# Second feed-forward stage: where the offset and scale of the middle layer norm are applied to the stored residual rows

## The chip, the cores and the metric

The kernel runs on one core of one Trainium2 chip. The metric is device microseconds (us) of one execution. The kernel before takes 2586.59 us (median of 3 runs, 2585.88 to 2588.91). In the text PE is TensorE, DVE is VectorE, ACT is ScalarE, POOL is GpSimd and SP is SyncE, whose queue issues all the DMAs that matter here.

## The reference, cut to what matters

One layer of a transformer-like backbone acts on 1152 rows (1024 latent tokens and 128 context tokens) of width 1024: a feed-forward part, a token mixer, a second feed-forward part, each closed by a layer norm over the residual.

```python
x = layer_norm(ALPHA * x + 0.5 * g1 * swiglu(x * (1.0 + sc1) + sh1, w_f1_in, w_f1_out), ln_g[0], ln_b[0])
y, aux = mixer(x * (1.0 + sc2) + sh2)
x = layer_norm(ALPHA * x + g2 * y, ln_g[1], ln_b[1])
x = layer_norm(ALPHA * x + 0.5 * g3 * swiglu(x * (1.0 + sc3) + sh3, w_f2_in, w_f2_out), ln_g[2], ln_b[2])
```

The change is about the third line and how its result reaches the fourth. Write z for the normalised row, (v - mean) / std. The layer norm's result is z * ln_g[1] + ln_b[1]. It is used twice: as the input of the second feed-forward (for which ln_g[1] and ln_b[1] are folded into per-column factors, so that the feed needs z alone), and as the residual ALPHA * x, which is needed only at the very end, when the last layer norm is made. Matrix products are made in float32 quality by splitting each operand in a high and a low float16 part ("hi" and "lo") and adding three products.

## The kernel before, in words

The 1152 rows are nine tiles (t = 0 to 8) of 128 rows in the buffer Y, 128 x 1024 float32 each. The program's third part (`ffn_phase` with the tag ffn2) begins with the mixer's output projection (class `MixOut`) and goes on with the second feed-forward. Each engine has its own instruction list, written out by hand; the order in a list is fixed, and semaphores are waited for by count. So an engine that waits holds back everything behind it in its own list.

**The opening.** PE makes the output projection tile by tile (L1600). DVE gates it, adds the residual, takes the statistics (`sums`), POOL makes 1/std (`pool`, L1767 and L1768), and DVE makes z in place (`unit`, L1705). PE turns z (L143), ACT and DVE scale it and split it into `act_hi` and `act_lo` (class `Feed`, L165, L170, L184). In between and afterwards, DVE applies the residual's scale and offset to z in place: `affine` (L1708 to L1715) makes two instructions a tile, z * gB (L1714) and + bB (L1715), where gB and bB are ALPHA * ln_g[1] and ALPHA * ln_b[1] spread over all partitions. Tile 0 is done in `vector`, tiles 1 to 5 between the parts of group 0, tiles 6 to 8 in group 1, between its second and third `product`. `store_rows` (L1563) then writes each tile to `x_after_2` in HBM; SP waits for `affined` before each store. Y is then free for the feed-forward's sums.

**The feed-forward.** The hidden width of 2816 is cut into 22 blocks of 128, two blocks (GB) to a group, eleven groups (NG). For each block PE multiplies all rows with two weight columns ("up", L2217 in groups 0 to 2 and 10; a scheme with fewer products, the quarter groups, L2310, in groups 3 to 9), ACT makes SiLU, DVE multiplies and takes maxima (`product`, L2718 and L125), and scales are found from the largest values (`hidden_max`, `hidden_scale`, `win_scale`). A group's "down" products (L2263) are made one group later, in 18 half tiles; DVE adds each to Y (`add`, L2751 for the first, L2753 for the others). Three PSUM banks serve the half tiles in turn, so PE can be three ahead of DVE's adds.

In group 1 PE's list is: up of block 2 for three column chunks, with `spread_h` and `spread_win` (L120) after the first one, which need DVE's `hidden_max` and `win_max` of what came before; `spread_win`; the down products of group 0; up of block 3. DVE's list for it is in `group` (L2760): win_max, product, hidden_scale, win_scale, hidden_lo (L2742), win_lo, product, `mix.affine(dve, 6, 7, 8)`, product, win_scale, and then the eighteen adds. In a quarter group (`quarter_group`, L2858) DVE runs joins (L2829), `low_pieces` (L2855), gates (L2836, L2843), the weights' low parts (L2677, L2673), `hidden_rows`, and the adds.

**POOL.** After the feed is split, POOL makes sums of the operands for the quarter groups (`sums`, L1979 to L2000), and then three instructions for each of the blocks 6 to 19 (`weight_sums`, L2013, L2016, L2019), each set waiting for the set of weights (`raw_in`), for `in_lo` of the block before and for `w_max`. ACT's `win_hi` (L2460) waits for them. At the end POOL gates and merges rows (`Ending.pool`).

**SP.** In each group (L2098) SP waits for `in_lo`, loads a block of input weights, stores rows if any, waits for the next `in_lo`, loads the next block, waits for `out_lo`, and loads two blocks of output weights. The rows of `x_after_2` are read again only in the last group (L1821). The gate rows of the ending are loaded in the opening (L1807).

Of the kernel before, what the change touches and what calls it, by code (L numbers as in the profile page):

```python
# [69 lines left out]
class Plan:  # L70


    def __init__(self, nc, base):
        self.nc, self.at = nc, base
# [117 lines left out]
class Modulation:  # L192
# [177 lines left out]
    def group(self, i):  # L370

        return self.K.mod[:, i * KT:(i + 1) * KT, :]
# [1163 lines left out]
class MixOut:  # L1536


    def __init__(self, K, nc, place, banks, w_at, row_at, feed_at, res_at):
        self.K, self.nc = K, nc  # L1540
# [10 lines left out]
        self.gate = place("mixout_gate_rows", [P, 2, D])  # L1551
        self.gB, self.bB = place("mixout_ln_g_rows", [P, D]), place("mixout_ln_b_rows", [P, D])
        self.xs = [fixed(f"residual_{i}", [P, D], res_at + 4096 * i) for i in range(2)]
# [6 lines left out]
        self.bn, self.rstd, self.z = sem("bn_done"), sem("rstd_done"), sem("z_done")  # L1560
        self.affined, self.x2_stored = sem("rows_affine"), [sem("rows_stored"), sem("last_rows_stored")]

    def store_rows(self, sp, *tiles):  # L1563

        for t in tiles:
            sp.wait_ge(self.affined, t + 1)
            sp.dma_start(self.K.x2_rows(t), self.K.Y[:, t, :]).then_inc(self.x2_stored[t // 6], 16)
# [139 lines left out]

    def affine(self, dve, *tiles):  # L1708

        Y = self.K.Y  # L1710
        for t in tiles:
            dve.wait_ge(self.feeds[t // 6].turned, KT if t // TPC != 1 else 2 * KT)
            dve.wait_ge(self.z, t + 1)
            self.link(self.nc.vector.tensor_tensor(Y[:, t, :], Y[:, t, :], self.gB[:], ALU.mult))  # L1714
            self.nc.vector.tensor_tensor(Y[:, t, :], Y[:, t, :], self.bB[:], ALU.add).then_inc(self.affined, 1)  # L1715

    def vector(self, dve, win_max, win_scale, win_lo):
# [12 lines left out]
        for c, t in ((0, 3), (1, 6)):  # L1730
            self.gated(dve, t, 0, 1)
            self.sums(dve, t)
            if c == 0:
                win_lo(0, 0)
                win_scale(1, 1)
            self.residual(dve, t + 1)
            self.unit(dve, t)
            rest(c, 0, 1)
            self.gated(dve, t + 1, 0)
            rest(c, 2, 3)  # L1740
            self.gated(dve, t + 1, 1)
            self.sums(dve, t + 1)
            rest(c, 4, 5)
            self.residual(dve, t + 2)
            self.unit(dve, t + 1)
            self.gated(dve, t + 2, 0)
            rest(c, 6, 7)
            if c == 0:
                win_lo(1, 1)
            self.gated(dve, t + 2, 1)  # L1750
            self.sums(dve, t + 2)
            self.residual(dve, t + 3)
            if c == 0:
                dve.wait_ge(self.affine_rows, 32)
                for rows in (self.gB, self.bB):
                    self.link(self.nc.vector.tensor_scalar(rows[:], rows[:], ALPHA, None, ALU.mult))
            else:
                self.affine(dve, 0)
            self.unit(dve, t + 2)
# [157 lines left out]


START = 3

# [116 lines left out]
def ffn_phase(nc, K, place, banks, tag, w_in, w_out, unit_i, first=False, out_dst=None):  # L2037

    with ExitStack() as ctx:
# [20 lines left out]
        hfac = place(f"{tag}_h_factor", [P, GB])  # L2060
        mod = qkv = att = end = mix = quarters = None
        if first:
# [5 lines left out]
        else:  # L2068
            end = Ending(K, nc, tag, place, 2, 8, out_dst, spare_at)
            mix = MixOut(K, nc, place, banks, wout_at, odd_at, odd_at + 4 * GB * TOK, end.gated_at)  # L2070
            quarters = Quarters(K, nc, tag, GB * START, GB * (NG - 1 - START), ((end.gated_at + 12288, end.gated_at + 16384), (end.rows_at, end.rows_at + 8192),
                                                              (mix.free_at + 16384, nc.sbuf_usable_end), (mix.free_at, mix.free_at + 8192), (mix.free_at + 8192, mix.free_at + 16384)), spare_at, end.gated_at)
        pa, pu, py = banks[0:2], banks[2:4], banks[4:7]
        h_all, w_all = banks[7][:, 0:P], [banks[7][:, P:2 * P], banks[7][:, 2 * P:3 * P]]
# [15 lines left out]
        def _(sp):  # L2090
# [6 lines left out]

            def group(i, early=(), rest=()):  # L2098
                sp.wait_ge(in_lo, i * GB + 2)
                load_in(i * GB + 3, 1)  # L2100
                mix.store_rows(sp, *early)
                sp.wait_ge(in_lo, i * GB + 3)
                load_in(i * GB + 4, 0)
                mix.store_rows(sp, *rest)
                sp.wait_ge(out_lo, i * GB + GB)
                for b in range(GB):
                    load_out(i * GB + (GB + b), b)

            def late(done):
# [44 lines left out]
            if mix:  # L2154
                end.load_gates(sp)
                mix.load_late(sp)
# [7 lines left out]
            if mix:  # L2164
# [3 lines left out]
                for b in range(GB):  # L2168
                    load_out(b, b)
                mix.store_rows(sp, 0, 1, 2, 3)  # L2170
            if mod:
# [5 lines left out]
            else:  # L2177
                group(0, rest=(4, 5))
                group(1, early=(6, 7, 8))
                for i in range(2, NG - 2):  # L2180
                    group(i)
            sp.wait_ge(in_lo, NB - 2)
# [10 lines left out]
            else:  # L2193
                sp.wait_ge(quarters.products, quarters.PER * quarters.blocks)
                end.load_rows(sp)
                end.load_residuals(sp)
                end.store(sp)
# [451 lines left out]
        def _(dve):  # L2649
# [110 lines left out]
            def group(i, par, n, fresh=False, last=False, at=None, late=None, brackets=False, rows=False):  # L2760
# [13 lines left out]
                product(i, par, 0, 1)  # L2774
                if rows:
                    mix.affine(dve, 6, 7, 8)
                product(i, par, 0, 2)
# [150 lines left out]
            def last_group(i):  # L2928
                tile = lambda t: end.tile(dve, t, 2 * end.POS["last", t], py, y_ready, y_added, (NG - 2) * HPG)
                row = lambda t: end.finish_row(dve, t)  # L2930
                dve.wait_ge(out_lo, NB - GB)
                dve.wait_ge(quarters.products, quarters.PER * quarters.blocks)
# [91 lines left out]
            else:  # L3024
                late = mix.feeds[1]
                mix.splits(dve)
                mix.vector(dve, win_max, win_scale, win_lo)
                dve.wait_ge(end.gates, 32)
                mix.affine(dve, 1)
                product(0, 0, 0, 0, n=0)  # L3030
# [3 lines left out]
                win_max(2, 0, 1)  # L3034
                mix.affine(dve, 2)
                product(0, 0, 0, 1, n=2)
                mix.affine(dve, 3, 4)
                product(0, 0, 0, 2, n=3)
# [4 lines left out]
                wout_lo(0)  # L3043
                mix.affine(dve, 5)
                product(0, 0, 1, 2, n=5)
# [14 lines left out]
        def _(gp):  # L3060
# [4 lines left out]
            else:  # L3065
# [5 lines left out]

                quarters.sums(gp, fed, lambda gp: gp.wait_ge(mix.affined, NT))
                for blk in range(quarters.first_block, GB * (NG - 1)):
                    quarters.weight_sums(gp, blk, wraw[blk % 2], raw_in[blk % 2], w_max, in_lo)
                end.pool(gp, y_added, (NG - 2) * HPG + 3)

# [921 lines left out]
```

## Time and profile before

| | us |
|---|---|
| median of 3 runs | 2586.59 |
| profiled execution | 2587.3 |
| its span, first to last instruction | 2585.6 |
| PE busy in the span | 2405.1 (93%) |
| DVE busy | 1934.9 (75%) |
| ACT busy | 876.0 (34%) |
| POOL busy | 421.5 (16%) |
| mean granted TensorE clock | 0.970 of full speed |

All positions are us from the span's start. The opening of the third part begins near 1668, its group 0 at 1776, group 1 at 1827, group 2 at 1920; the quarter groups 3 to 9 follow every 65.7 us from 1990.7, and group 10 with the ending fills 2452 to 2586. The span is 1.7 us shorter than the time of the execution.

### The profile page before, as it was taken

To read this page: it belongs to the slowest core of one execution; us is meant where nothing else is said; L and a number is where in the kernel's file an instruction comes from. 1 tells how busy PE (TensorE), PEld (TensorE's weight loads), DVE (VectorE), ACT (ScalarE), POOL (GpSimd) and SP (SyncE) were. 2 spreads that over 40 slices of the span, in tenths; PEclk is the share of its full clock that TensorE was granted. 3 is DMA by queue.
4 is the path that set the end of the run, shared out by engine and by line. 5 is a ranking of instruction groups with operands and counts; after the bars stand their busy time and mean duration, and the time that the engine had idled before them with its cause. 6 is when DMAs were issued, how large, how long until landed. Compare 5 with 4: busy or idle time off the path is not lost. (4 is left out here: it accounts for less than half of the span.)

```text
span 2585.6 us, 38871 instructions
## 1 busy us (share of the span) xinstructions
PE 2405.1 (93%) x15844; PEld 1522.7 (59%) x15844; DVE 1934.9 (75%) x2925; ACT 876.0 (34%) x1431; POOL 421.5 (16%) x354
## 2 busy tenths in 40 slices
PE   7999999999999787999889999799799999999986
PEld 2555555655555476777667776545455666666643
DVE  3687777788676776888747778898966777777787
ACT  2511111111121344777644554623212333333220
POOL 0000000000000012222200010312941111111047
PEclk9999999999999898999989999899899999999998
DMA  9123223321303110000021111131311111111112
GB/s 334 50 98 100 97 82 98 115 98 49 98 17 95 57 54 6 22 1 1 17 65 32 37 51 38 65 109 58 114 33 49 50 50 50 50 50 50 54 45 98
DMA packets 153715, 170.53 MB, mean 66 GB/s; under 512 B 12055, under 2 KB 128691, under 8 KB 152514
## 3 DMA queue, kind: packets, MB, share of 16 engines
q1 hardware_dynamic: 153538, 168.05, 20.1%
q8 instruction: 126, 2.06, 0.3%
q14 instruction: 51, 0.42, 0.1%
HBM read 153.18 MB, written 14.84 MB: 65 GB/s over the span
## 5 line engine op out<-in xcount | busy, mean ns | idle before, releaser
L2217 PE MATMUL psum<-act_hi,ffn_win_hi 128*128 128x384 f16 x1392 | 454.8, 327 | 3.7 <-DVE ffn_win_lo L2685 2.4
L2217 PE MATMUL psum<-act_lo,ffn_win_hi 128*128 128x384 f16 x1392 | 454.8, 327 | 0.0
L2217 PE MATMUL psum<-act_hi,ffn_win_lo 128*128 128x384 f16 x1392 | 454.6, 327 | 0.0
L2484 ACT ACTIVATE ffn_silu<-psum,ffn_win_inverse 128x384 f32<-128x384 f32 x90 | 52.2, 580 | 729.7 <-PE psum L2217 726.6
L2263 PE MATMUL psum<-ffn_wout_hi,ffn_h_hi 128*128 128x512 f16 x720 | 278.7, 387 | 19.4 <-DVE Y L2751 12.0
L2753 DVE SCALAR_TENSOR_TENSOR Y<-psum,ffn_h_unit,Y 128x512 f32<-128x512 f32 x306 | 225.2, 749 | 82.9 <-PE psum L2263 82.3
L2263 PE MATMUL psum<-ffn_wout_lo,ffn_h_hi 128*128 128x512 f16 x720 | 278.0, 386 | 0.0
L2263 PE MATMUL psum<-ffn_wout_hi,ffn_h_lo 128*128 128x512 f16 x720 | 277.3, 385 | 0.0
L2217 PEld LDWEIGHTS psum<-act_hi,ffn_win_hi 128*128 128x128 f16 x1392 | 136.5, 98 | 94.4 <-issue 2.8
L2217 PEld LDWEIGHTS psum<-act_hi,ffn_win_lo 128*128 128x128 f16 x1392 | 136.5, 98 | 90.5 <-issue 0.8
L2217 PEld LDWEIGHTS psum<-act_lo,ffn_win_hi 128*128 128x128 f16 x1392 | 136.5, 98 | 89.9 <-issue 0.7
L993 POOL TENSOR_SCALAR ffn_rstd<-ffn_meanvar 128x1 f32<-128x1 f32 x9 | 2.0, 225 | 926.6 <-DVE ffn_meanvar L899 926.5
L2460 ACT ACTIVATE ffn_win_hi<-ffn_win_raw,ffn_win_scale 128x2048 f16<-128x2048 f32 x44 | 87.8, 1996 | 189.4 <-DVE ffn_win_inverse L2665 92.8
L2263 PEld LDWEIGHTS psum<-ffn_wout_hi,ffn_h_hi 128*128 128x128 f16 x720 | 71.5, 99 | 112.8 <-DVE Y L2751 12.9
L3338 PE MATMUL psum<-act_hi,scan_w_hi 128*128 128x384 f16 x384 | 125.4, 326 | 0.0
L3338 PE MATMUL psum<-act_lo,scan_w_hi 128*128 128x384 f16 x384 | 125.2, 326 | 0.0
L3338 PE MATMUL psum<-act_hi,scan_w_lo 128*128 128x384 f16 x384 | 125.2, 326 | 0.0
L2263 PEld LDWEIGHTS psum<-ffn_wout_hi,ffn_h_lo 128*128 128x128 f16 x720 | 71.6, 99 | 88.4 <-issue 6.1
L430 DVE SCALAR_TENSOR_TENSOR mod_sums<-w_mod,silu_cond,mod_sums 128x1024 f32<-128x1024 f32 x98 | 122.8, 1277 | 0.0
L1344 DVE TENSOR_REDUCE score_min<-psum 128x1 f32<-128x1280 f32 (+1 forms) x72 | 97.5, 1355 | 33.1 <-PE psum L1137 22.3
L1356 DVE TENSOR_TENSOR probsT_lo<-psum,probsT_hi 128x512 fp32r<-128x512 f32 x162 | 105.7, 684 | 19.7 <-ACT probsT_hi L1275 19.5
L2263 PEld LDWEIGHTS psum<-ffn_wout_lo,ffn_h_hi 128*128 128x128 f16 x720 | 71.5, 99 | 81.8 <-issue 4.9
(425 smaller groups left out, 5577.6 us busy)
## 6 DMA issues: line engine op xcount, KB each, us to landing
ffn_win_raw<-in_w_in SPq DMA_DIRECT2D x88, 512.0 KB, 5.1
w_mod<-in_w_mod SPq DMA_DIRECT2D x36, 1024.0 KB, 4.8
ffn_wout_raw<-in_w_out SPq DMA_DIRECT2D x44, 512.0 KB, 4.1
scan_w_raw<-in_w_mix SPq DMA_DIRECT2D x20, 512.0 KB, 5.4
x_after<-Y SPq DMA_DIRECT2D x18, 512.0 KB, 2.6
mixout_residual<-x_after SPq DMA_DIRECT2D x9, 512.0 KB, 3.4
ffn_residual<-x_after SPq DMA_DIRECT2D x9, 512.0 KB, 3.4
Y<-in_x_sample SPq DMA_DIRECT2D x8, 512.0 KB, 11.7
```

The costliest lines, as they stand in the source:

```text
L430: ins = nc.vector.scalar_tensor_tensor(acc, w, factor, acc, ALU.mult, ALU.add)
L993: link(nc.gpsimd.tensor_scalar(self.rs[:, t:t + 1], self.mv[:, t, 1:2], EPS, None, ALU.add))
L1344: self.nc.vector.tensor_reduce(self.low[:, u % 2, s:s + 1], self.score_view(u, s), AX_X, ALU.min).then_inc(self.s_min, 1)
L1356: nc.vector.tensor_tensor(self.pt[g % self.NPT][1][:], self.T[i % 2], self.pt[g % self.NPT][0][:].bitcast(F32), ALU.subtract).then_inc(sel ...
L2217: last = nc.tensor.matmul(bank[:, 0:CH], win[b][w][:, half, k, :], K.A[a][:, k, c * CH:(c + 1) * CH], start=(n == 0), stop=(n == 3 * KT - 1))
L2263: last = nc.tensor.matmul(py[m % 3], h[a][:, b, t * P:(t + 1) * P], wout[w][:, b, 0, half * 512:(half + 1) * 512], start=(n == 0), stop=(n ...
L2460: nc.scalar.activation(win[par][0][:], wraw[par][:], ACT.Copy, scale=ws[:, par:par + 1]).then_inc(in_hi, 1)
L2484: nc.scalar.activation(sa[s][:], pa[s][:, 0:CH], ACT.Silu, scale=winv[:, b:b + 1]).then_inc(silu, 1)
L2753: ins = nc.vector.scalar_tensor_tensor(dst, py[m % 3], hq[:], dst, ALU.mult, ALU.add)
L3338: last = nc.tensor.matmul(proj[u % 2][:, 0:CH], w[x][:, k, :], K.A[y][:, k, i * CH:(i + 1) * CH], start=(m == 0), stop=(m == 3 * KT - 1))
```

## The change

DVE's eighteen `affine` instructions are taken out, and z itself is stored in `x_after_2`. Because the stores no longer wait for `affined` but for z, SP issues six of them right after the output projection and three in group 0. A new class `Pieces` then reads each tile back from HBM in two halves of 128 x 512 (18 pieces), POOL multiplies and adds (two instructions a piece, 36 in all), and SP stores the piece where it came from. There is one piece buffer, so load, multiply, add and store of a piece follow one another, and a piece's load waits until the store of the one before has landed. Pieces are spread over the groups 2 to 7, three a group: SP's waits and issues stand in `group` after each of its three loads, POOL's instructions after each `weight_sums` (one piece for an even block, two for an odd one). The buffers gB and bB move to where the ending's gate rows are, and so live until the last piece; the gate rows are therefore loaded after group 8 and no longer in the opening, and DVE's wait for them moves from the opening to the last group. POOL's `sums` no longer wait for `affined` (their last operand buffers lay on gB and bB) but for the output projection's rows.

```diff
     def store_rows(self, sp, *tiles):
 
         for t in tiles:
-            sp.wait_ge(self.affined, t + 1)
+            sp.wait_ge(self.z, t + 1)
             sp.dma_start(self.K.x2_rows(t), self.K.Y[:, t, :]).then_inc(self.x2_stored[t // 6], 16)
...
-    def affine(self, dve, *tiles):
-
-        Y = self.K.Y
-        for t in tiles:
-            dve.wait_ge(self.feeds[t // 6].turned, KT if t // TPC != 1 else 2 * KT)
-            dve.wait_ge(self.z, t + 1)
-            self.link(self.nc.vector.tensor_tensor(Y[:, t, :], Y[:, t, :], self.gB[:], ALU.mult))
-            self.nc.vector.tensor_tensor(Y[:, t, :], Y[:, t, :], self.bB[:], ALU.add).then_inc(self.affined, 1)
...
+class Pieces:
...
+    COUNT = 2 * NT
...
+    def finish(self, sp, n):
+
+        sp.wait_ge(self.made, n + 1)
+        sp.dma_start(self.home(n), self.piece[:]).then_inc(self.stored, 16)
+
+    def turn(self, sp, *numbers):
+
+        for n in numbers:
+            if n:
+                self.finish(sp, n - 1)
+                sp.wait_ge(self.stored, 16 * n)
+            else:
+                sp.wait_ge(self.sums_made, Quarters.KH)
+                sp.wait_ge(self.mix.x2_stored[0], 96)
+                sp.wait_ge(self.mix.x2_stored[1], 48)
+            sp.dma_start(self.piece[:], self.home(n)).then_inc(self.loaded, 16)
+
+    def affine(self, gp, *numbers):
+
+        for n in numbers:
+            cols = slice(n % 2 * (D // 2), (n % 2 + 1) * (D // 2))
+            gp.wait_ge(self.loaded, 16 * n + 16)
+            self.nc.gpsimd.tensor_tensor(self.piece[:], self.piece[:], self.mix.gB[:, cols], ALU.mult).then_inc(self.multiplied, 1)
+            gp.wait_ge(self.multiplied, n + 1)
+            self.nc.gpsimd.tensor_tensor(self.piece[:], self.piece[:], self.mix.bB[:, cols], ALU.add).then_inc(self.made, 1)
...
-            def group(i, early=(), rest=()):
+            def group(i, turns=(), rest=()):
                 sp.wait_ge(in_lo, i * GB + 2)
                 load_in(i * GB + 3, 1)
-                mix.store_rows(sp, *early)
+                if turns:
+                    pieces.turn(sp, *turns[0])
                 sp.wait_ge(in_lo, i * GB + 3)
                 load_in(i * GB + 4, 0)
                 mix.store_rows(sp, *rest)
+                if turns:
+                    pieces.turn(sp, *turns[1])
                 sp.wait_ge(out_lo, i * GB + GB)
                 for b in range(GB):
                     load_out(i * GB + (GB + b), b)
+                if turns:
+                    pieces.turn(sp, *turns[2])
...
             if mix:
-                end.load_gates(sp)
                 mix.load_late(sp)
...
-                mix.store_rows(sp, 0, 1, 2, 3)
+                mix.store_rows(sp, 0, 1, 2, 3, 4, 5)
...
-                group(0, rest=(4, 5))
-                group(1, early=(6, 7, 8))
+                group(0, rest=(6, 7, 8))
+                group(1)
                 for i in range(2, NG - 2):
-                    group(i)
+                    n = 3 * (i - 2)
+                    turns = () if n >= pieces.COUNT else ((), (n,), (n + 1, n + 2)) if i == 2 else ((n,), (n + 1,), (n + 2,))
+                    group(i, turns)
+                pieces.finish(sp, pieces.COUNT - 1)
+                end.load_gates(sp)
...
                 for blk in range(quarters.first_block, GB * (NG - 1)):
                     quarters.weight_sums(gp, blk, wraw[blk % 2], raw_in[blk % 2], w_max, in_lo)
+                    n = 3 * ((blk - quarters.first_block) // GB)
+                    if n < pieces.COUNT:
+                        pieces.affine(gp, *((n + 1, n + 2) if blk % 2 else (n,)))
```

## Rows read from the trace of the kernel before

**Rows 1.** The page, its slices: PE's busy tenths and granted clock in 40 slices.

```profile
PE   7999999999999787999889999799799999999986
PEclk9999999999999898999989999899899999999998
```

**Rows 2.** PE's waits, 1776 to 1930: who it waited for, total, times, longest.

```profile
PE psum L2263 <- DVE Y L2751: 12.0, 1, 12.0
PE psum L120 <- DVE ffn_h_top L2726: 3.2, 1, 3.2
PE psum L120 <- DVE ffn_win_row_max L125: 1.7, 1, 1.7
PE psum L2217 <- DVE ffn_h_even L2718: 0.5, 1, 0.5
```

**Rows 3.** By line: the eighteen affine instructions; min/median/max ns, first and last start.

```profile
L1714 DVE TENSOR_TENSOR Y<-Y,mixout_ln_g_rows x9: 1177/1744/2420, 1780.2 to 1865.9; 128x1024 f32<-128x1024 f32 x9
L1715 DVE TENSOR_TENSOR Y<-Y,mixout_ln_b_rows x9: 1224/2180/2309, 1781.4 to 1868.2; 128x1024 f32<-128x1024 f32 x9
```

**Rows 4.** Timeline of DVE, 1842 to 1874: start, length, instruction.

```profile
1842.11 0.61 DVE L2718 SCALAR_TENSOR_TENSOR ffn_h_odd<-psum,ffn_win_inverse,ffn_silu 128x384 f32<-128x384 f32 x1
...
1858.59 1.22 DVE L1714 TENSOR_TENSOR Y<-Y,mixout_ln_g_rows 128x1024 f32<-128x1024 f32 x1
...
1870.44 0.60 DVE L2718 SCALAR_TENSOR_TENSOR ffn_h_odd<-psum,ffn_win_inverse,ffn_silu 128x384 f32<-128x384 f32 x1
```

**Rows 5.** The chain of waits, 1820 to 1905, and 1940 to 1990: start, length, what.

```profile
1873.92 0.76 DVE Y L2751
1874.73 21.82 PE psum L2263 x90
...
1944.01 23.31 PE psum L2263 x108
1967.32 22.75 PE psum L2217 x140
```

**Rows 6.** Stretches: busy us and count of each engine, granted clock, DMA.

```profile
1840.00:1845.00 5.00, 4.94 (x16) 2.64 (x17) 4.76 (x10) 0.19 (x1) 4.69 (x5) 0.50 0.21 84
1875.00:1880.00 5.00, 5.00 (x15) 1.82 (x14) 1.99 (x4) 0.92 (x1) 4.69 (x5) 0.57 0.00 0
```

**Rows 7.** Timeline of ACT, 1805 to 1840: SiLU of unit 6.

```profile
1834.67 0.58 ACT L2484 ACTIVATE ffn_silu<-psum,ffn_win_inverse 128x384 f32<-128x384 f32 x1 [5.97 <-PE psum L2217]
```

**Rows 8.** By line: POOL's 128x512 addition, DVE's low parts and adds; min/median/max ns.

```profile
L2016 POOL TENSOR_TENSOR ffn_w_sums<-ffn_win_raw,ffn_w_sums x14: 1266/1276/2202, 1940.9 to 2380.5; 128x512 f32<-128x512 f32 x14
L2742 DVE SCALAR_TENSOR_TENSOR ffn_h_lo<-ffn_h_even,ffn_h_factor,ffn_h_hi x42: 609/615/1752, 126.1 to 1852.5; 128x384 f16<-128x384 f32 x42
L2753 DVE SCALAR_TENSOR_TENSOR Y<-psum,ffn_h_unit,Y x306: 740/750/752, 214.1 to 2430.2; 128x512 f32<-128x512 f32 x153
```

**Rows 9.** Timeline of DVE in quarter group 4, 2056 to 2123.

```profile
2066.95 1.68 DVE L2855 SCALAR_TENSOR_TENSOR ffn_h_lo<-ffn_h_odd,ffn_h_factor,ffn_h_hi 128x384 f16<-128x384 f32 x3 [1.59 <-ACT ffn_h_hi L2474]
...
2072.32 0.52 DVE L2829 SCALAR_TENSOR_TENSOR ffn_h_even<-psum,ffn_win_inverse,ffn_h_even 128x288 f32<-128x288 f32 x1 [0.36 <-ACT ffn_h_even L2517]
2074.66 0.52 DVE L2829 SCALAR_TENSOR_TENSOR ffn_h_even<-psum,ffn_win_inverse,ffn_h_even 128x288 f32<-128x288 f32 x1 [1.82 <-PE psum L2310]
...
2111.01 2.33 DVE L2677 SCALAR_TENSOR_TENSOR ffn_win_lo<-ffn_win_raw,ffn_win_scale,ffn_win_hi 128x2048 f16<-128x2048 f32 x1
```

**Rows 10.** The chain of waits in the same group: PE goes on with the down products.

```profile
2084.62 17.06 PE psum L2263 x78
```

**Rows 11.** Timeline of SP, 2018 to 2121: DMA issues.

```profile
2083.93 32.17 SPq L2093 DMA_DIRECT2D ffn_win_raw<-in_w_in  x4
```

**Rows 12.** The page, DMA issues: KB each, median us to landing.

```profile
ffn_win_raw<-in_w_in SPq DMA_DIRECT2D x88, 512.0 KB, 5.1
x_after<-Y SPq DMA_DIRECT2D x18, 512.0 KB, 2.6
mixout_residual<-x_after SPq DMA_DIRECT2D x9, 512.0 KB, 3.4
```

More of the change, by code:

```diff
@@ L1536, with __init__ @@
 class MixOut:
-    def __init__(self, K, nc, place, banks, w_at, row_at, feed_at, res_at):
+    def __init__(self, K, nc, place, banks, w_at, row_at, feed_at, res_at, affine_at):
         self.K, self.nc = K, nc
@@ L1551, in __init__ @@
         self.gate = place("mixout_gate_rows", [P, 2, D])
-        self.gB, self.bB = place("mixout_ln_g_rows", [P, D]), place("mixout_ln_b_rows", [P, D])
+        self.gB, self.bB = fixed("ln_g_rows", [P, D], affine_at), fixed("ln_b_rows", [P, D], affine_at + 4096)
         self.xs = [fixed(f"residual_{i}", [P, D], res_at + 4096 * i) for i in range(2)]
@@ L1560, in __init__ @@
         self.bn, self.rstd, self.z = sem("bn_done"), sem("rstd_done"), sem("z_done")
-        self.affined, self.x2_stored = sem("rows_affine"), [sem("rows_stored"), sem("last_rows_stored")]
+        self.scaled_rows, self.x2_stored = sem("ln_rows_scaled"), [sem("rows_stored"), sem("last_rows_stored")]
     def store_rows(self, sp, *tiles):
         for t in tiles:
-            sp.wait_ge(self.affined, t + 1)
+            sp.wait_ge(self.z, t + 1)
             sp.dma_start(self.K.x2_rows(t), self.K.Y[:, t, :]).then_inc(self.x2_stored[t // 6], 16)
@@ L1755, in vector @@
                 for rows in (self.gB, self.bB):
-                    self.link(self.nc.vector.tensor_scalar(rows[:], rows[:], ALPHA, None, ALU.mult))
-            else:
-                self.affine(dve, 0)
+                    self.nc.vector.tensor_scalar(rows[:], rows[:], ALPHA, None, ALU.mult).then_inc(self.scaled_rows, 1)
             self.unit(dve, t + 2)
@@ L1916, in finish_row, with __init__, home @@
         self.nc.vector.scalar_tensor_tensor(Y[:, t, :], Y[:, t, :], self.rs[:, t:t + 1], self.bB[:], ALU.mult, ALU.add).then_inc(self.row_done, 1)
+class Pieces:
+    COUNT = 2 * NT
+    def __init__(self, K, nc, mix, sums_made, at):
+        self.K, self.nc, self.mix, self.sums_made = K, nc, mix, sums_made
+        self.piece = nc.alloc_sbuf_tensor_at("residual_piece", [P, D // 2], F32, offset=at)
+        self.loaded, self.multiplied, self.made, self.stored = (K.semaphore(f"residual_piece_{n}") for n in ("loaded", "multiplied", "made", "stored"))
+    def home(self, n):
+        return self.K.x2_rows(n // 2)[:, n % 2 * (D // 2):(n % 2 + 1) * (D // 2)]
+    def finish(self, sp, n):
[18 more added lines that the diff above has]
+            self.nc.gpsimd.tensor_tensor(self.piece[:], self.piece[:], self.mix.bB[:, cols], ALU.add).then_inc(self.made, 1)
 START = 3
@@ L2060, in ffn_phase @@
         hfac = place(f"{tag}_h_factor", [P, GB])
-        mod = qkv = att = end = mix = quarters = None
+        mod = qkv = att = end = mix = quarters = pieces = None
         if first:
@@ L2069, in ffn_phase @@
             end = Ending(K, nc, tag, place, 2, 8, out_dst, spare_at)
-            mix = MixOut(K, nc, place, banks, wout_at, odd_at, odd_at + 4 * GB * TOK, end.gated_at)
+            mix = MixOut(K, nc, place, banks, wout_at, odd_at, odd_at + 4 * GB * TOK, end.gated_at, end.gated_at - 8192)
             quarters = Quarters(K, nc, tag, GB * START, GB * (NG - 1 - START), ((end.gated_at + 12288, end.gated_at + 16384), (end.rows_at, end.rows_at + 8192),
                                                               (mix.free_at + 16384, nc.sbuf_usable_end), (mix.free_at, mix.free_at + 8192), (mix.free_at + 8192, mix.free_at + 16384)), spare_at, end.gated_at)
+            pieces = Pieces(K, nc, mix, quarters.made, spare_at + 6144)
         pa, pu, py = banks[0:2], banks[2:4], banks[4:7]
@@ L2195, in _ @@
                 end.load_rows(sp)
+                sp.wait_ge(pieces.stored, 16 * pieces.COUNT)
                 end.load_residuals(sp)
@@ L2774, in group @@
                 product(i, par, 0, 1)
-                if rows:
-                    mix.affine(dve, 6, 7, 8)
                 product(i, par, 0, 2)
@@ L2930, in last_group @@
                 row = lambda t: end.finish_row(dve, t)
+                dve.wait_ge(end.gates, 32)
                 dve.wait_ge(out_lo, NB - GB)
@@ L3027, in _ @@
                 mix.vector(dve, win_max, win_scale, win_lo)
-                dve.wait_ge(end.gates, 32)
-                mix.affine(dve, 1)
                 product(0, 0, 0, 0, n=0)
@@ L3034, in _ @@
                 win_max(2, 0, 1)
-                mix.affine(dve, 2)
                 product(0, 0, 0, 1, n=2)
-                mix.affine(dve, 3, 4)
                 product(0, 0, 0, 2, n=3)
@@ L3043, in _ @@
                 wout_lo(0)
-                mix.affine(dve, 5)
                 product(0, 0, 1, 2, n=5)
@@ L3070, in fed @@
                     gp.wait_ge(mix.feeds[1].lo, KT)
-                quarters.sums(gp, fed, lambda gp: gp.wait_ge(mix.affined, NT))
+                quarters.sums(gp, fed, lambda gp: gp.wait_ge(mix.y_taken, 2 * NT))
+                gp.wait_ge(mix.scaled_rows, 2)
                 for blk in range(quarters.first_block, GB * (NG - 1)):
                     quarters.weight_sums(gp, blk, wraw[blk % 2], raw_in[blk % 2], w_max, in_lo)
+                    n = 3 * ((blk - quarters.first_block) // GB)
+                    if n < pieces.COUNT:
+                        pieces.affine(gp, *((n + 1, n + 2) if blk % 2 else (n,)))
                 end.pool(gp, y_added, (NG - 2) * HPG + 3)
```

## The prediction

> **What bounds the kernel now.** I read the slices of the page first, then PE's waits in the thin slices, then the chain of waits through them, then the timelines of the engines that it names. PE is busy in nine tenths or more of most slices; the thinner ones before the last are the start and the places where a stage changes [rows 1]. The slices are 64.6 us each, so the 28th (1745 to 1810) and the 29th and 30th (1810 to 1939) hold the opening and group 1; the 29th shows 7 tenths for PE and 8 for its clock. There PE waits four times, each time for DVE: 12.0, 3.2, 1.7 and 0.5 us, 17.4 in all [rows 2]. After two of the waits the granted clock is at its lower level of 1.2 GHz for some 4 us (0.50 and 0.57 of full speed as means over 5 us), and PE starts 16 and 15 matmuls in 5 us [rows 6], where the chain has one per 0.1625 us of the up kind and one per 0.216 us of the down kind at the full 2.4 GHz [rows 5]. That costs 4.94 - 16 x 0.1625 = 2.3 us after the first pause. After the second, 90 down matmuls took 21.82 us where 90 x 0.216 is 19.4, so 2.4 us.
>
> DVE has all eighteen affine instructions in exactly this stretch, 1780.2 to 1870.5 [rows 3], at 1.74 and 2.18 us median. The long wait is read off the timeline: product of unit 7 ends at 1858.59, then the six instructions for tiles 6, 7, 8 run until the product of unit 8 starts at 1870.44 [rows 4], 11.85 us; the first add to Y can only come at 1873.92, and PE's down products go on at 1874.73 [rows 5]. From group 2 to group 9 PE is without a gap of note. So this is a kernel that is bound by PE, except in a stretch of about 50 us in which DVE's list is.
>
> **The change part by part.**
>
> *Group 0, tiles 0 to 5 taken off DVE.* Twelve affine instructions go. The waits of 0.5, 3.2 and 1.7 us are DVE being late with the product of unit 4, hidden_max and win_max. What is late next? Unit 6 (the first of group 1) now starts 0.5 earlier, so its SiLU comes at 1834.67 - 0.50 = 1834.17 and ends at 1834.75 [rows 2, 7]. DVE has shed about 20 us by then, so hidden_max and both win_max are ready before. PE runs on without its pauses of 3.2 and 1.7 us. The input weights for it are not late either: SP was held at its four stores for tile 0 to 3, and these now go out at once.
>
> *Group 1, tiles 6 to 8 taken off.* DVE's own list becomes the limit from 1834.75. From product 6 to the end of product 7 it took 1858.59 - 1842.11 = 16.48 us [rows 4], with POOL's sums beside it, as after the change. From product 8 to the first add it took 1873.92 - 1870.44 = 3.48 us, and the add with its hand-over 0.81. So the fourth half tile's bank is free at 1834.75 + 16.48 + 3.48 + 0.81 = 1855.5. PE is there at 1834.2 + 0.7 for the spreads + 15.6 for two units + 3.9 for three half tiles = 1854.4, so a wait of about 1.1 us stays. The other 90 matmuls take 90 x 0.216 = 19.4 us instead of 21.82 [rows 5], since the clock has no pause of 12 us to fall after. Down products of group 0 end at 1855.5 + 19.4 = 1874.9 instead of 1874.73 + 21.82 = 1896.55: **21.6 us earlier**. The other way round: 17.4 of waits and 4.7 of clock are 22.1, less the 1.1 that stays, 21.0. Bounds: 21.0 by this count, 22.7 if DVE is 1.1 us faster than before. I take 21.6, the sum along the list. That DVE sheds 18 x (1.74 to 2.18), some 35 us, and PE gets 22 says that the rest was already hidden.
>
> *Everything after* shifts with PE, since each group waits for nothing that has a fixed time. POOL's sums start at the same place, and are needed only by the first quarter group, over a group after they end.
>
> *The 36 POOL instructions.* The nearest row is POOL's addition of the same shape: 1.27 us, up to 2.20 when DVE is at it too [rows 8]. Three pieces a group are 6 x 1.27 = 7.6 us, on an engine that is idle for 84% of the span. Their own time costs nothing. What can cost is DVE. A DVE instruction with two SBUF inputs goes from 0.61 to as much as 1.75 us with POOL active (low parts), while the adds that read PSUM stay within 740 to 752 ns in all 306 [rows 8].
>
> The Trainium skill ("SBUF — State Buffer", section "Who interferes with whom") has it that a DVE instruction with two SBUF inputs and a GpSimd instruction that reads SBUF exclude each other for a whole instruction, and that one with at most one SBUF input is left alone. The trace agrees with both halves, by the 1752 and the 752 just named.
>
> So each of the two instructions of a piece may hold back one DVE instruction by up to 1.27 us. It reaches PE only inside one stretch: from the join at 2074.66, which DVE itself awaited PE for (1.82 us idle) [rows 9], to PE's going on at 2084.62 [rows 10]. Before it DVE has 0.36 + 1.82 = 2.2 us to spare. Where do the pieces fall? First piece of a group: after the weight load at 2083.93 [rows 11] lands (5.1), store (at most 2.6) and load (at most 3.4, both for double the size) [rows 12], 2090 to 2096, among the adds: nothing. Second: SP is past its second load at 2116.1 [rows 11]; load lands 2121, store by 2123.3, piece by 2125 to 2127, POOL 2.6 us; in this group's phase (less 65.7) 2059.5 to 2064, among maxima and joins: nothing. Third: store and load again, 3.4 to 6.8 us, so it starts at 2065.3 to 2071 and ends at 2068 to 2073.6, on the low parts before the stretch. Two blocked instructions are 2.54 us against 2.2 to spare: 0 to 0.35 a group. Times six groups, 0 to 2; I take 1.5. The far bound is the third piece wholly inside the stretch, 6 x 2.54 = 15.2.
>
> *SP.* A `turn` holds SP for a store's landing, 3 us, ahead of the output weights' load; these are wanted in the second half of the next group. The next input load stands behind the last turn of the group, which ends near 2131 where its own wait ends at 2149.6. Hidden, by 18 us. If not, each us late there would be one on `win_max`.
>
> *Gate rows.* Loaded near 2370 for use near 2455; nothing. gB, bB and the first turn's waits: long fulfilled.
>
> **Sum.** 2587.3 (profiled, span 2585.6 plus 1.7) - 21.6 + 1.5 = 2567.2. The median of the runs shown is 0.7 below the profiled one: **2566.5 us**.
>
> **The rivals.**
>
> A, the third piece falls into the stretch: DMAs are slower beside two loads of 512 KB than their medians; 2 to 7 us would do. 2586.6 - 21.6 + 15.2 = 2580.2; half of it 2572.6. For it: the chain store, load, POOL, store, load has five links. Against it: the medians are for twice the bytes. 14%.
>
> B, something else in the opening is late next (ACT's feed, the output weights behind six stores of 512 KB), and only the 12 us wait with its clock goes, less 1.1: 12.0 + 2.4 - 1.1 = 13.3, so 2586.6 - 13.3 + 1.5 = 2574.8. Against it: PE had no wait for ACT or a DMA anywhere in it [rows 2]. 8%.
>
> C, the other side: POOL's pieces hold DVE wherever they are, since DVE's list in a quarter group is in fact tight. Every one of 36 instructions then costs its 1.27: 45.7 us, 2586.6 - 21.6 + 45.7 = 2610.7. It is slower from 17 of the 36 on. For it: at the end of the stretch the chain passes from DVE to PE [rows 10]. Against it: DVE idles three times in the 10 us before the stretch [rows 9], so only what falls in 10 of 65.7 us can count. 4%.
> The Trainium skill ("Perfetto Trace Analysis", section "Optimizing Scalar/DVE Operations") speaks for C: it warns that shifting work between GpSimd and DVE may not help because of the port they share. The traces bear it out for the low parts only.
>
> **How the numbers follow.** The forecast has 74%, with its own range 2564.5 to 2570. The range reaches down to 2562.5 (22.7 gained, nothing paid, some 1.4 for what I don't see) and up over B to 2576. About 0.2% or 5.2 us is what can be told from no change, so faster means under 2581.4: the forecast, B and nearly all of A, 94%; same 3%; slower 3%.
>
> **What would show it.** PE's waits between 1776 and 1930 should be one of about 1 us in place of 17.4, the granted clock 1.00 throughout, and down products of group 0 end near 1875. Quarter groups should repeat every 65.7 to 66.1 us; 67 and more would be A, 72 C. POOL's third piece should start 3 to 9 us before the join that PE releases. The prediction is wrong if PE still waits for over 4 us in the opening, or if a quarter group grows by more than 1 us.

## The result, and the profile after

The changed kernel takes 2564.14 us (median of 4 runs, 2560.20 to 2566.49), the kernel before 2586.24 (4 runs of the same session): the ratio is 0.9907, 95% interval 0.9894 to 0.9920, so 20.7 to 27.4 us less. The forecast was a gain of 20.1 us, a time of 2566.5 with 2564.5 to 2570 as the range of its own mechanism, and 2562.5 as the lowest time thought possible. The gain came, and more of it than forecast: the median of 2564.14 lies 2.4 us below the forecast and 0.4 below its own range, and 0.9907 of 2586.59 us is 2562.5, at the lowest edge. A second session of the same kernel gave 0.9912 (0.9896 to 0.9927). So the whole time tells the gain to some 3 us either way, and the stages have to tell the rest.

The page of the kernel after, the same slices as [rows 1]: the 29th slice, which showed 7 and 8 tenths, shows 9 and 9.

```profile
PE   7999999999999787999879999889999999999987
PEclk9999999999999898999989999899999999999998
```

PE's waits in 1770 to 1930, one line in place of the four of [rows 2]:

```profile
PE psum L2303 <- DVE Y L2791: 0.2, 1, 0.2
```

The opening and group 1 before and after, 1776 to 1930 (busy us and counts of PE, PEld, DVE, ACT and POOL, granted clock, DMA). The granted clock is 1.00 after the change, and it was 0.93:

```profile
1776.00:1930.00 154.00, 136.56 (x784) 78.65 (x783) 118.88 (x131) 31.26 (x50) 103.88 (x70) 0.93 0.24 79
...
1776.00:1930.00 154.00, 153.83 (x911) 89.78 (x909) 101.13 (x145) 40.60 (x64) 95.65 (x73) 1.00 0.27 86
```

The chain of waits through the same place (start, length, what), which answers to [rows 4, 5]. Lines have moved by 40 in this part of the kernel.

```profile
1838.50 0.63 DVE ffn_h_odd L2758
...
1842.28 8.24 DVE ffn_h_lo L2782 x6
...
1854.95 0.63 DVE ffn_h_odd L2758
...
1857.10 0.17 DVE ffn_win_inverse L2705
...
1857.29 0.76 DVE Y L2791
1858.10 19.60 PE psum L2303 x90
```

From product 6 to product 8 DVE takes 16.45 us, as the 16.48 before, and the low parts are still at 8.2 us with POOL's sums beside them. The six affine instructions that stood before 1854.95 are gone. The 90 matmuls take 19.6 us. The one line that the forecast had otherwise is `ffn_win_inverse`, an instruction on 128 x 1 values, which takes 0.17 us. Before, it took 1.33 us and ended with POOL's instruction that had begun just ahead of it (chain, then POOL's timeline):

```profile
1872.57 1.33 DVE ffn_win_inverse L2665
...
1872.47 1.40 POOL L1979 TENSOR_TENSOR ffn_a_sum_tmp<-ffn_a_sum_tmp,ffn_a_sum_tmp 128x576 f32<-128x576 f32 x1
```

To compare stages across runs I take landmarks from PE's timeline: the first matmul of the output projection, the first up matmul of group 0, the first up matmul behind the down products of group 0, the first and the last matmul of the quarter groups, and the end. Each length is a difference of two starts, in us.

| run | projection at | opening | to quarters | quarter groups | rest |
|---|---|---|---|---|---|
| before | 1668.2 | 120.0 | 94.2 | 459.9 | 135.1 |
| before, again | 1669.0 | 120.1 | 94.2 | 459.9 | 132.1 |
| after | 1672.1 | 97.4 | 94.2 | 459.9 | 132.5 |
| after, again | 1669.6 | 97.4 | 94.2 | 459.9 | 133.9 |
| no_pieces | 1671.9 | 97.4 | 94.2 | 459.9 | 132.4 |
| pool_x9_first | 1672.1 | 97.4 | 94.2 | 460.2 | 132.4 |
| stretch | 1666.9 | 97.4 | 94.2 | 476.0 | 134.7 |
| less_678 | 1671.8 | 106.0 | 94.2 | 459.9 | 135.0 |
| less_0to5 | 1672.5 | 112.9 | 94.2 | 459.9 | 134.9 |
| late_sums | 1671.5 | 99.1 | 99.0 | 459.9 | 133.9 |
| late_sums_k1 | 1672.0 | 105.8 | 95.5 | 459.9 | 136.0 |
| gated_early | 1668.0 | 97.4 | 94.2 | 459.9 | 132.3 |
| gated_pool | 1672.1 | 97.4 | 94.2 | 459.9 | 132.3 |

The projection itself is 108.0 to 108.4 in all. The opening, the way to the quarters and the quarter groups repeat within 0.1 us for one kernel. The first and the last column do not: over all profiles they vary by 5.6 and 3.9 us, and by 0.8 and 3.0 between the two profiles of the kernel before, 2.5 and 1.5 between the two of the changed kernel. The gain is in the opening: 120.05 - 97.4 = 22.65 us.

What the prediction named as its signs can be read here. PE's waits fell to 0.2 us, the quarter groups repeat every 65.7 us, and the down products of group 0 end at 1877.7 where the first up matmul of group 0 stands at 1780.2. In the kernel before that matmul stood 3.8 earlier, so this is 1873.9 on its scale, 1.0 before the forecast of 1874.9.

### The profile page after: what moved, and what is told of

It is laid out like the page before. It is cut to its first block and busy times, and to the rows that moved or that the text cites. A ratio compares the mean times of both kernels' runs of the same rounds, so it can differ in the third digit from the quotient of the medians.

```text
span 2564.1 us, 38920 instructions
## 1 busy us (share of the span) xinstructions
PE 2404.4 (94%) x15844; PEld 1522.7 (59%) x15844; DVE 1909.9 (74%) x2907; ACT 875.2 (34%) x1431; POOL 454.9 (18%) x390
```

## The experiments

**The changed kernel again, for the spread.**

> The changed kernel once more. Theory T: the gain is made of 22.7 us in the opening (down products of group 0 end 97.5 us after the first up matmul of group 0, 120.2 before), nothing in the quarter groups (65.7 us each in both), and some 2.7 us in the last group that belong to no edit and will vary from run to run. Then the ratio is 0.990 to 0.992, and the last group takes 124 to 128 us in this run. Rival R: the 2.7 us come from the edit (gate rows at another time, POOL in another phase), and the last group takes 124.4 again in every run of this kernel.

Measured 0.9912 (0.9896 to 0.9927), 2565.33 us. Its opening and quarter groups are the same to 0.1; its rest is 133.9, and 132.5 in the first profile. R, the rival by which the last group takes the same time in every run of this kernel, falls.

**The kernel before again.**

> The kernel before once more, for the spread of its stages from run to run. T: opening 120.2 us from the first up matmul of group 0 to the end of its down products, within 0.5; last group 124 to 128 us. R (the last group's 2.7 us belong to the edit): 127.1 within 0.3 again.

Measured 0.9997 (0.9987 to 1.0007) against itself. The rest was 132.1 here and 135.1 in the first profile: 3.0 us between two executions of one program. So the 2.7 us between the two first profiles are no more than the spread, and R falls here too. Over all profiles the rest has a mean of 134.5 in the six that keep some or all of the affine instructions on DVE and 132.9 in the seven others, and the two sets overlap; whether 1 to 2 us belong to the edit stays open.

**Without the pieces.** The edit: no `turn`, no `affine` on POOL; the last residual is then z without scale and offset.

```diff
-                    turns = () if n >= pieces.COUNT else ((), (n,), (n + 1, n + 2)) if i == 2 else ((n,), (n + 1,), (n + 2,))
+                    turns = ()
...
-                pieces.finish(sp, pieces.COUNT - 1)
...
-                    if n < pieces.COUNT:
+                    if False:
```

> The changed kernel without the eighteen pieces: no loads, no POOL multiply and add, no stores back, so the last residual is z without scale and offset. T: pieces are free; same time within 1 us, quarter groups 65.7 us. Forecast of the prediction: 1.5 us faster. Rival A or C: 7 to 15 us faster, or more.

Measured 0.9904 (0.9887 to 0.9921), 2564.23 us beside the 2565.33 of the changed kernel in the same session; quarter groups 459.9 in both. The pieces cost nothing that can be seen, not even the 1.5 us of the forecast.

It is not that POOL leaves DVE alone. Over the quarter groups DVE is busy 357.3 us with the pieces and 347.3 without them, for the same 537 instructions, so the pieces hold DVE for 10 us in all (changed kernel, then without the pieces; DVE is the third column):

```profile
1971.00:2432.00 461.00, 458.95 (x3156) 307.43 (x3153) 357.30 (x537) 146.34 (x224) 112.29 (x70) 1.00 0.21 66
...
1971.00:2432.00 461.00, 458.67 (x3154) 307.39 (x3152) 347.29 (x537) 146.43 (x224) 69.55 (x37) 1.00 0.16 48
```

In the changed kernel's timelines of POOL and DVE one sees where these go. This is a third piece (POOL), and what DVE does around it (start, length, instruction, idle before):

```profile
2049.22 1.69 POOL L1944 TENSOR_TENSOR residual_piece<-residual_piece,mixout_ln_g_rows 128x512 f32<-128x512 f32 x1 [5.51 <-DMA residual_piece<-x_after]
2050.99 1.27 POOL L1946 TENSOR_TENSOR residual_piece<-residual_piece,mixout_ln_b_rows 128x512 f32<-128x512 f32 x1
```

```profile
2051.02 0.52 DVE L2867 SCALAR_TENSOR_TENSOR ffn_h_even<-psum,ffn_win_inverse,ffn_h_even 128x288 f32<-128x288 f32 x1 [1.24 <-ACT ffn_h_even L2557]
2051.45 2.28 DVE L2893 SCALAR_TENSOR_TENSOR ffn_h_lo<-ffn_h_odd,ffn_h_factor,ffn_h_hi 128x384 f16<-128x384 f32 x3
2053.65 0.51 DVE L2867 SCALAR_TENSOR_TENSOR ffn_h_even<-psum,ffn_win_inverse,ffn_h_even 128x288 f32<-128x288 f32 x1
2055.82 0.52 DVE L2867 SCALAR_TENSOR_TENSOR ffn_h_even<-psum,ffn_win_inverse,ffn_h_even 128x288 f32<-128x288 f32 x1 [1.66 <-PE psum L2350]
```

The second group of low parts takes 2.28 us. In the kernel before, the same three instructions took

```profile
2070.30 1.67 DVE L2855 SCALAR_TENSOR_TENSOR ffn_h_lo<-ffn_h_odd,ffn_h_factor,ffn_h_hi 128x384 f16<-128x384 f32 x3
```

so DVE is held for 0.6 us. It then still idles 1.66 us before the join that PE releases at 2055.82. The piece runs 6.6 to 3.6 us ahead of that join. Of the 2.2 us to spare, 0.6 are used. The six third pieces start 12.4, 6.6, 8.3, 8.0, 8.2 and 8.8 us ahead of their joins; the prediction had said 3 to 9.

**The third piece put into the stretch.** The edit: POOL waits for the join.

```diff
             gp.wait_ge(self.loaded, 16 * n + 16)
+            if n % 3 == 2:
+                gp.wait_ge(self.joined, 12 * (n // 3 + 0) + 5)
...
+            pieces.joined = quarters.joined
```

> The changed kernel, with POOL's work on each third piece held until DVE has made the join that PE releases in the next quarter group, so that its multiply and add run inside the ten microseconds in which DVE's list sets PE. The theory of the prediction (price 2.54 us for each such piece, six of them): 15 us slower than the changed kernel, quarter groups 68.2 us. Rival: a held DVE instruction costs only what is left of POOL's when it comes, 0.6 us each on average: 3 to 8 us. Rival that the port never matters: 0.

Measured 0.9976 (0.9966 to 0.9985), 2582.87 us, 17.5 above the changed kernel in the same session. The quarter groups take 476.0 instead of 459.9: 16.1 us in six groups. The two rivals (3 to 8 us, and 0) fall. First POOL, then DVE, then PE in one of the groups:

```profile
2054.49 1.35 POOL L1946 TENSOR_TENSOR residual_piece<-residual_piece,mixout_ln_g_rows 128x512 f32<-128x512 f32 x1 [12.95 <-DVE ffn_h_even L2870]
2055.92 1.36 POOL L1948 TENSOR_TENSOR residual_piece<-residual_piece,mixout_ln_b_rows 128x512 f32<-128x512 f32 x1
```

```profile
2054.62 1.53 DVE L2884 SCALAR_TENSOR_TENSOR ffn_h_even<-ffn_h_even,ffn_first_product 128x288 f32<-128x288 f32 x1
2056.07 3.35 DVE L2720 SCALAR_TENSOR_TENSOR ffn_win_lo<-ffn_win_raw,ffn_win_scale,ffn_win_hi 128x2048 f16<-128x2048 f32 x1
```

```profile
2062.82 0.39 PE L2306 MATMUL psum<-ffn_wout_hi,ffn_h_hi 128*128 128x512 f16 x1 [1.99 <-DVE Y L2796]
```

Two DVE instructions are held, 1.53 us where they take 0.45 and 3.35 where they take 2.34, 2.1 together, and PE waits 1.99 instead of 0.28 at its fourth half tile. The same pause of 1.99 us stands in each of the six groups. The rest is the clock. These are 4 us at each of the six pauses or just behind it (busy us and counts of each engine, granted clock, DMA):

```profile
1994.00:1998.00 4.00, 4.00 (x12) 1.50 (x11) 3.93 (x7) 0.00 (x0) 1.69 (x1) 0.57 0.07 19
2062.00:2066.00 4.00, 2.90 (x13) 1.21 (x14) 3.99 (x5) 0.00 (x0) 0.71 (x1) 1.00 0.00 0
2130.00:2134.00 4.00, 3.38 (x9) 1.19 (x10) 4.00 (x5) 0.00 (x0) 0.91 (x1) 0.58 0.00 0
2199.00:2203.00 4.00, 3.11 (x14) 1.30 (x15) 4.00 (x5) 0.00 (x0) 0.92 (x1) 1.00 0.00 0
2267.00:2271.00 4.00, 3.31 (x15) 1.39 (x16) 4.00 (x6) 0.00 (x0) 1.12 (x1) 1.00 0.02 5
2335.00:2339.00 4.00, 3.79 (x10) 1.39 (x11) 4.00 (x6) 0.00 (x0) 1.32 (x1) 0.57 0.03 6
```

After the pause the clock fell to its 1.2 GHz level in three of the six groups and stayed at 2.4 GHz in the other three. From one block of up matmuls to the next, the down products take 23.9 us in the changed kernel, 26.0 here where the clock stayed and 27.2 where it fell. So 2.1 us a group, 12.5 in all, are DVE held, and the other 3.5 are the clock. The theory had 2.54 us a piece, 15 in all, from the holding alone: its sum comes near because the two instructions were held for less than their whole length and the clock, which it did not count, made up for it.

**POOL made busy elsewhere.** The edit: the multiplication of each first piece nine times, which spoils the residual of those pieces.

```diff
-            self.nc.gpsimd.tensor_tensor(self.piece[:], self.piece[:], self.mix.gB[:, cols], ALU.mult).then_inc(self.multiplied, 1)
+            extra = 8 if n % 3 == 0 else 0
+            for r in range(1 + extra):
+                self.nc.gpsimd.tensor_tensor(self.piece[:], self.piece[:], self.mix.gB[:, cols], ALU.mult).then_inc(self.multiplied, 1)
...
```

> The changed kernel, with the multiplication of each first piece of a group made nine times (48 more POOL instructions of 128x512, 10.7 us more in each of six groups, among DVE's adds; the residual of those pieces is then wrong). T: only what falls in the ten critical microseconds costs, so 0 to 1 us. Rival C (POOL holds DVE wherever it is): 48 x 1.27 = 61 us.

Measured 0.9920 (0.9906 to 0.9934), 2567.17 us; quarter groups 460.2 instead of 459.9. So 48 POOL instructions more, 62 us of POOL's time, cost 0.3 us, and rival C falls. In POOL's timeline the nine of one group stand in a row, 12.06 us or 1.34 each with the gaps between them, while DVE makes its adds:

```profile
2075.37 12.06 POOL L1946 TENSOR_TENSOR residual_piece<-residual_piece,mixout_ln_g_rows 128x512 f32<-128x512 f32 x9 [5.12 <-DMA residual_piece<-x_after]
```

**Half of the change, one way.** The kernel before, with one call less; the stores of these tiles wait for z, and their residual is left without scale and offset.

```diff
                 product(i, par, 0, 1)
-                if rows:
-                    mix.affine(dve, 6, 7, 8)
```

> The kernel before without the affine instructions of tiles 6 to 8 alone (their residual is then z without scale and offset). Prediction's steps: the wait of 12.0 us in group 1 and the clock after it go, the three waits in group 0 stay (0.5, 3.2, 1.7, and 2.3 of clock). DVE is later than PE by what is left, so the gain is near the six instructions, 11.9 us, and 2.3 of clock: 14 us. Rival: half, 6 to 8, if another wait comes up behind.

Measured 0.9942 (0.9925 to 0.9959), 2573.0 us; the opening is 106.0, 14.0 us shorter, as expected. The three waits of group 0 stay, and the long one is down to 0.2:

```profile
PE psum L120 <- DVE ffn_h_top L2726: 3.2, 1, 3.2
PE psum L120 <- DVE ffn_win_row_max L125: 1.7, 1, 1.7
PE psum L2217 <- DVE ffn_h_even L2718: 0.5, 1, 0.5
PE psum L2263 <- DVE Y L2751: 0.2, 1, 0.2
```

**Half of the change, the other way.** The kernel before without the other calls; again the stores of these tiles wait for z, and their residual is left without scale and offset.

```diff
-            else:
-                self.affine(dve, 0)
...
-                mix.affine(dve, 1)
...
-                mix.affine(dve, 2)
...
-                mix.affine(dve, 3, 4)
...
-                mix.affine(dve, 5)
```

> The kernel before without the affine instructions of tiles 0 to 5 alone. Prediction's steps: the waits of 0.5, 3.2 and 1.7 us and 2.3 of clock go, 7.7 us; since DVE's list bounds the way to the 12 us wait too, that wait grows by what DVE does not gain: DVE's product of unit 6 comes at 1834.7 instead of 1842.1, 7.4 us. Gain 7 to 8 us. Rival: less than 3, since PE only reaches the 12 us wait earlier.

Measured 0.9969 (0.9956 to 0.9982), 2578.46 us; the opening is 112.9, 7.1 us shorter. The three waits are gone and the long one grew from 12.0 to 13.2:

```profile
PE psum L2264 <- DVE Y L2752: 13.2, 1, 13.2
```

PE reaches this wait 8.6 us earlier and stays 1.2 us longer in it, since DVE gained less than PE, and the 90 matmuls behind it take 0.4 us more. 7.1 us stay, and the rival (under 3) falls. The two halves give 14.0 + 7.1 = 21.1; together they give 22.65.

**Nothing taken off DVE, but POOL kept silent.** The kernel before; one wait more ahead of POOL's sums.

```diff
                     gp.wait_ge(mix.feeds[1].lo, KT)
+                    gp.wait_ge(y_added, 5)
```

> The kernel before, nothing left out, with POOL's operand sums held until the first two adds of group 1, so that POOL is silent while DVE makes the affine instructions. Theory P: much of the loss in the opening was the port, not the instructions: eighteen affine instructions took 35 us where they take 22 undisturbed, the low parts 8.3 where 3.3; PE's 17.4 us of waits shrink by 10 or more, and the kernel is 9 to 14 us faster. Rival: the instructions themselves are the loss; under 4 us. It loses if the sums (80 us undisturbed, from 1875) are late for the first quarter group at 1991.

Measured 0.9934 (0.9919 to 0.9948), 2570.99 us: 17 us faster than before, with every affine instruction still on DVE, and more than the 9 to 14 expected. The opening is 99.1, 21.0 us shorter of the 22.65 that the whole change brings. By line, the two affine lines of [rows 3] and the low parts (min/median/max ns, first and last start):

```profile
L1714 DVE TENSOR_TENSOR Y<-Y,mixout_ln_g_rows x9: 1178/1219/1225, 1783.6 to 1853.9; 128x1024 f32<-128x1024 f32 x9
L1715 DVE TENSOR_TENSOR Y<-Y,mixout_ln_b_rows x9: 1224/1225/1227, 1784.8 to 1855.1; 128x1024 f32<-128x1024 f32 x9
L2742 DVE SCALAR_TENSOR_TENSOR ffn_h_lo<-ffn_h_even,ffn_h_factor,ffn_h_hi x42: 608/614/619, 126.2 to 1844.2; 128x384 f16<-128x384 f32 x42
```

Eighteen instructions at 1.22 us are 22 us, and they all but fit beside PE: one wait of 1.9 us is left in the opening. What PE waited for in the kernel before was DVE held by POOL, in these and in the instructions around them. PE's waits from 1770 to 2020 in this kernel:

```profile
PE psum L2217 <- DVE ffn_h_even L2718: 3.0, 1, 3.0
PE psum L2263 <- DVE Y L2751: 1.9, 1, 1.9
PE psum L2263 <- DVE Y L2753: 0.5, 2, 0.3
```

The 3.0 us and the lower clock after it (0.76 as a mean over 1965 to 1972) are most of the 4.9 us by which the stage before the quarters is longer. It isn't the quarter groups that wait for the sums, as I had expected. POOL's `weight_sums` of block 6 stand behind the sums in its list, ACT's `win_hi` of that block waits for them,

```profile
ACT ffn_win_hi L2460 <- POOL ffn_win_raw L2019: 31.1, 1, 31.1
```

and the SiLUs of group 2 stand behind `win_hi` in ACT's list.

**A part of the sums early.** The same, with the first of the four steps of the sums made at once and three held.

```diff
+            if k == 1:
+                held(gp)
             if k == self.KH - 1:
                 rows_done(gp)
```

> The kernel before, nothing left out; POOL makes the first quarter of its operand sums at once and holds only the other three until the first adds of group 1. The held sums of the last experiment shortened the opening by 21.0 us and then made the first quarter group wait 4.9 us. Here the sums end some 20 us sooner, so that wait goes; the opening loses what DVE is held in 1799 to 1826: affine of tiles 2 to 4 in contention, 5 us on DVE, of which PE sees 0 to 5. Expected 15 to 21 us faster than before; rival: the early sums cost PE more than 5 us.

Measured 0.9955 (0.9939 to 0.9972), 2576.79 us, 11.6 faster than before by the ratio. The opening is 105.8, so the one early step costs PE 6.7 us, and the rival is right; the 15 to 21 us expected did not come. The stage before the quarters is now 1.3 us longer than in the kernel before, where it was 4.9 longer in the last experiment.

**Two tries for a faster kernel.** Both start from the changed kernel and move the gated product of the second block of output weights in the last group: the first on DVE to an idle place, the second to POOL.

```diff
...
                 wout_rows(i, 0, gated=True)
+                dve.wait_ge(out_in[1], i * 16 + 16)
+                link(nc.vector.tensor_tensor(end.gated[:, 1], oraw[1][:].unsqueeze(1).broadcast_to([P, 2, D]), end.gate[:], ALU.mult))
```

> A further step on the changed kernel, nothing left out: in the last group DVE makes the gated product of the second block of output weights (2.28 us) before the first product, where it idles 1.6 us, and not between win_lo and the maximum. By the chain of waits of the changed kernel the product comes 0.65 us later and the maximum 2.28 earlier: last group 1.6 us shorter, where it varied by 3 us from run to run; the time 1.6 us below the changed kernel. Rival: PE's wait for win_lo grows by 0.65 and nothing else moves: 0.6 us slower.

```diff
...
+                gp.wait_ge(end.even_gated, 1)
+                nc.gpsimd.tensor_tensor(end.gated[:, 1], oraw[1][:].unsqueeze(1).broadcast_to([P, 2, D]), end.gate[:], ALU.mult).then_inc(end.odd_gated, 1)
                 end.pool(gp, y_added, (NG - 2) * HPG + 3)
```

> The same step with the gated product of the second block made by POOL (128x2048, some 4.7 us by its 2.35 us for 128x1024), after DVE has made the first one: DVE's list loses 2.28 us and the product is not late. 2.3 us below the changed kernel. Rival: POOL's instruction is held by or holds DVE's low parts (two SBUF operands), and the gain is 0 to 1.

Measured 0.9903 (0.9889 to 0.9916), 2561.59 us, and 0.9915 (0.9902 to 0.9928), 2565.64 us. Neither differs from the changed kernel (0.9907 and 0.9912), and the rest of 132.3 in both is among the values seen without them. With the product early on DVE, PE's wait of 2.8 us at the first chunk's maximum is gone and its wait for `win_lo` grew from 2.4 to 3.1, as the rival had it; but the mean granted clock from 2425 to 2560 was 0.91 where it was 0.95 in the changed kernel's first profile, and the rest came out the same. With the product on POOL, the wait at the first chunk's maximum fell from 2.8 to 0.5, but the wait before the last tiles was 6.6 and not 4.3:

```profile
PE psum L2288 <- DVE ffn_last_h_lo L2960: 6.6, 1, 6.6
...
PE psum L120 <- DVE ffn_chunk_top L2946: 0.5, 1, 0.5
```

That later wait was 6.6 in the first profile of the kernel before and 4.3 in its second one; in the changed kernel it was 4.3 first and then 6.6. So neither value belongs to the edit. What decides between them was not tried.

## Why the prediction was right or wrong

*The place and the mechanism: right.* The four waits and the clock were the loss; tiles 6 to 8 and tiles 0 to 5 split it as said (14.0 and 7.1, expected in the two experiments as 14 and 7 to 8); what follows shifted, to 0.1 us in each stage up to the last group. The forecast failed by the size of two terms, both of the same sign.

*The step "product 8 to the first add, 3.48 us": this is where the opening was mis-sized.* The prediction carried it over as it stood and left a wait of 1.1 us. It measured 2.34, and the wait 0.2. The 1.14 us between them are the one small instruction at 1.33 us, which had run beside a POOL instruction of 1.40 us and now took 0.17. A small part goes the other way: the 90 matmuls took 19.6 us and not 19.4. The opening gained 22.65, not 21.6; the upper bound of 22.7 had covered just this, "if DVE is 1.1 us faster", though it gave no reason why DVE might be. Whether so small an instruction meets one of POOL is decided anew by each shift: it took 1.32 us in the kernel before and without tiles 0 to 5, 0.56 without tiles 6 to 8, and 0.16 in both profiles of the changed kernel and with POOL's sums held back.

*The step "0 to 0.35 a group, I take 1.5": too much.* The right value was 0.0, from two runs with and without the pieces. The prediction let both instructions of a third piece hold DVE for their whole 2.54 us against 2.2 to spare. Measured, the third piece shown above held DVE for 0.6 us and 1.66 of idle time stayed; over the quarter groups the pieces held it for 10 us, some 0.3 an instruction, and PE saw none of it. The far bound of 15.2 was a little low: putting the piece there cost 16.1, 12.5 of it DVE held and 3.5 the clock, which the bound had left out.

*The rest of the kernel: 0 in the forecast.* It may hold 1 to 2 us, within its own spread of 3, and is not settled.

Together: 21.6 - 1.5 = 20.1 was forecast, 22.65 - 0.0 is what the stages show, and 20.7 to 27.4 and 18.9 to 26.9 what the two ratios do. 2586.59 - 22.65 is 2563.9, and the median was 2564.14. Both missed terms have the same sign, which is why the time came out below the forecast's own range.

*The cause behind the waits: half seen.* The prediction knew that the affine instructions took 1.74 and 2.18 us in the kernel before and that POOL was beside them, and it counted the contention only as a price of the new pieces. It never asked what the old loss would be without it. The run with POOL's sums held back gives the answer: 21.0 of the 22.65 us in the opening go with POOL's silence alone. So DVE's list was too long for the opening mainly because POOL held it.

The Trainium skill's rule in "SBUF — State Buffer" ("Who interferes with whom") on two SBUF inputs is borne out by stretch, where two such instructions were held by 1.08 and 1.01 us, and by pool_x9_first, where the adds with one SBUF input were not (739 to 754 ns in all 306). The Trainium skill's warning in "Perfetto Trace Analysis" ("Optimizing Scalar/DVE Operations") did not decide here, since the 10 us for which the pieces held DVE fell in its idle time.

## What to carry to other kernels

When an engine's instructions take nearly twice their shortest time in the stretch that bounds a kernel, ask first who holds them, and try to move that one; here one wait on POOL gave 21.0 of the 22.65 us that moving eighteen instructions gave in the opening, though it lost 4.9 us later. Work moved to an engine that can hold another one costs by where it lands: six pieces cost 16 us inside a critical stretch of 10 us, and nothing where they ended 3.6 us or more ahead of it. A step carried over from the old trace carries its held instructions with it: compare each duration with the shortest of the same line. And compare stages by landmarks: the middle ones repeated to 0.1 us while the runs of one kernel spread by up to 9.

## What the runs showed of the hardware

A pause of 2.0 us on PE, otherwise busy, was followed by the lower granted clock in three of six like groups and not in the other three. A DVE multiplication or addition of 128x1024 with both inputs in SBUF took 1.22 us with POOL silent and up to 2.42 with POOL at its sums, and a DVE instruction on 128x1 values 1.33 instead of 0.17; POOL's own 128x576 instructions went from 1.27 to 2.13 us at the same time, so both sides pay.
